# A hybrid mixer and MLP block on one Trainium2 core: two pairs of activation sums kept in SBUF, and another order of the steps at gate/up's begin

## The reference, cut to what matters

```python
D_MODEL, SEQ, D_FF = 2048, 512, 5632
h = rmsnorm(x, norm_mix)
proj = h @ w_in                       # then an SSD mixer, a sparse attention, a short conv
x = x + concatenate([y_ssd, y_att, y_sc]) @ w_out
h2 = rmsnorm(x, norm_ffn)
g = causal_dwconv(h2 @ ffn_w_gate, ffn_conv_w)        # width 3
x = x + (silu(g) * (h2 @ ffn_w_up)) @ ffn_w_down
# rmsnorm(x, g) = x * rsqrt(mean(x * x) + 1e-6) * g
```

## Time and profile before

| | us |
|---|---|
| median of 3 runs | 2159.3 (2154.16 to 2162.18) |
| the profiled execution | 2157.02, of it span 2155.2 |
| TensorE busy | 2124.2 |
| VectorE busy | 1495.8 |
| GpSimd busy | 1294.1 |
| ScalarE busy | 1009.0 |

### The profile page before, as it was taken

One profiled execution on the slowest core, in us unless ns is written; L12 is line 12 of the kernel. 1 busy time (PEld: TensorE's weight loads), 2 busy tenths in 40 slices (PEclk: granted clock), 3 DMA queues, 4 the chain that ended last, 5 costly groups with the idle time before them and its releaser, 6 DMA issues.

```text
span 2155.2 us, 36413 instructions
## 1 busy us (share of the span) xinstructions
PE 2124.2 (99%) x12484; PEld 1844.4 (86%) x12484; DVE 1495.8 (69%) x2530; ACT 1009.0 (47%) x1474; POOL 1294.1 (60%) x730
## 2 busy tenths in 40 slices
PE   8999999999999999999999999999999899999999
PEld 6777777887888887888888888888888889999999
DVE  6489565677763226888888888888888756566665
ACT  6343334434333445545555555455555444444444
POOL 4445334454554655667767767677677566666565
PEclk9999999999999999999999999999999999999999
DMA  5324223333334543353544544545445885566544
GB/s 194 86 79 120 66 69 98 94 105 91 100 103 126 147 142 127 124 170 132 172 154 141 165 151 147 169 133 175 149 141 169 320 278 178 176 219 203 188 125 143
DMA packets 153613, 316.22 MB, mean 147 GB/s; under 512 B 13176, under 2 KB 57912, under 8 KB 153496
## 3 DMA queue, kind: packets, MB, share of 16 engines
q1 hardware_dynamic: 103552, 252.23, 36.2%
q10 hardware_dynamic: 49944, 62.45, 9.2%
HBM read 265.31 MB, written 49.18 MB: 146 GB/s over the span
## 4 chain that ended last, share of the span: by engine, by line
PE 87%; DVE 8%; DMA 2%; issue 1%; ACT 1%; POOL 0%; ACTq 0%; SPq 0%; DVEq 0%; POOLq 0%
PE ps L846 26%; PE ps L845 13%; PE ps L657 9%; PE ps L659 8%; PE ps L658 8%; PE ps L852 6%; PE ps L854 6%; PE ps L853 6%; DMA act_lo<-tlo 1%; DVE work L1402 1%; DVE work L1401 1%; DVE work L1305 1%; PE ps L753 1%; PE ps L739 0%; DVE work L1304 0%
## 5 line engine op out<-in xcount | busy, mean ns | idle before, releaser
L846 PE MATMUL ps<-comb,fhi 128*128 128x512 f32 x2464 | 862.1, 394 | 0.0
L612 POOL TENSOR_TENSOR flo<-raw,fhi 128x1024 fp32r<-128x1024 f32 (+2 forms) x252 | 486.5, 1935 | 376.1 <-ACT fhi L1160 372.6
L845 PE MATMUL ps<-comb,flo 128*128 128x256 f32 x2464 | 693.5, 281 | 4.7 <-DVE ps L1737 3.3
L582 POOL TENSOR_TENSOR wlo<-raw,whi 128x512 fp32r<-128x512 f32 x260 | 375.7, 1458 | 393.4 <-ACT whi L959 342.7
L846 PEld LDWEIGHTS ps<-comb,fhi 128*128 128x128 f32 x2464 | 462.3, 188 | 105.4 <-issue 0.2
L845 PEld LDWEIGHTS ps<-comb,flo 128*128 128x128 f32 x2464 | 466.2, 189 | 8.6 <-issue 4.2
L612 POOL TENSOR_TENSOR flo<-sum,fhi 128x1024 fp32r<-128x1024 f32 (+2 forms) x168 | 323.4, 1931 | 51.4 <-ACT fhi L1160 49.6
L1160 ACT ACTIVATE fhi<-ps 128x1024 fp32r<-128x1024 f32 (+2 forms) x168 | 141.6, 843 | 414.3 <-DVE ps L1620 258.9
L852 PE MATMUL ps<-comb,fhi 128*128 128x256 f32 x1120 | 319.2, 285 | 10.5 <-POOL flo L612 6.5
L657 PE MATMUL ps<-hhi,whi 128*128 128x512 f32 x784 | 319.5, 407 | 3.2 <-DVE hlo L1542 3.2
L854 PE MATMUL ps<-comb,fhi 128*128 128x256 f32 x1120 | 318.6, 284 | 0.0
(11 more groups left out here) (223 smaller groups left out, 3082.8 us busy)
## 6 DMA issues: line engine op xcount, KB each, us to landing
raw<-w_gu SPq DMA_DIRECT2D x176, 512.0 KB, 3.7
raw<-w_in SPq DMA_DIRECT2D x196, 256.0 KB, 3.1
raw<-w_dn SPq DMA_DIRECT2D x96, 256.0 KB, 3.1
raw<-w_dn SPq DMA_DIRECT2D x64, 320.0 KB, 3.0
act_hi<-thi ACTq DMA_DIRECT2D x22, 896.0 KB, 4.2
act_lo<-tlo ACTq DMA_DIRECT2D x22, 896.0 KB, 8.3
raw<-w_out SPq DMA_DIRECT2D x64, 256.0 KB, 3.2
comb<-act_hi SPq DMA_DIRECT2D x28, 512.0 KB, 3.9
```

Source lines behind the costliest of these rows:

```text
L582: nc.gpsimd.tensor_tensor(wlo[:, slot % NW, 0:width], raw[:, slot % NRAW, 0:width], whi[:, slot % NW, 0:width].bitcast(F32), ALU.subtract) ...
L612: nc.gpsimd.tensor_tensor(flo[s][:, 0:w], src[:, 0:w], fhi[s][:, 0:w].bitcast(F32), ALU.subtract).then_inc(f_lo_pool, 1)
L845: nc.tensor.matmul(dst[:, 0:HT], flo[s][:, w], both[:, HI, :], start=fresh and k == 0, stop=False, skip_group_check=True)
L846: ins = nc.tensor.matmul(dst, fhi[s][:, w], both, start=False, stop=k == n - 1, skip_group_check=True)
```

## The change

At gate/up's begin:
- the Newton step keeps its intermediate in the PSUM bank `MLP`, where its input lies, in place of `upv`; the wait for the stored x2 tiles moves from there to just ahead of L1735;
- the activation table of Ln and Exp is loaded after the high part of position 3 of unit 0, six instructions earlier;
- the splits of the last tile are cut in two: T2 alone, then the weight sum S2 of unit 0 (position 2), then T3 and T4, on ScalarE and on VectorE. The semaphore counts of GpSimd's `low_h2` and of TensorE's position 4 follow.

Pairs 20 and 21:
- chunk 0 is made of pairs 0, 1, 2 and 20, chunk 1 of 3, 4, 5, 21 and 6; the others follow (`PAIRS`), and the weights are laid out in the same order;
- pair 20 stays in `thi` and `tlo` through chunk 0, and TensorE reads it there; pair 21 is split straight into slot 7 of `comb` and `comb6`, and is there for chunk 1. Neither is stored nor loaded, nor is a landed store waited for in unit 45. The loads of chunks 0 and 1 bring 3 pairs in place of 4 beside `fifth`;
- as `thi` and `tlo` are in use longer, the x2 tiles 12 and 13 go to `x2d` (where `gpad` was), 14 to `upv` and 15 to `sqsum`; `load_x2(6)` and `load_x2(7)` wait for the last activation in place of the last stores, and are three DMAs in place of two.

```diff
-PAIR0 = [0, 4, 9, 13, 18]
+PAIRS = [[0, 1, 2, 20], [3, 4, 5, 21, 6], [7, 8, 9, 10], [11, 12, 13, 14, 15], [16, 17, 18, 19]]
...
+        def pieces(c, b):
+            half, pairs = 4 * (c % 2), PAIRS[c]
+            run = [m for m in pairs[:4] if m < FP - 2]
+            found = [(block_of(b)[:, part, half:half + len(run), :], store[b, :, run[0]:run[0] + len(run), :])
+                     for part, store in ((HI, act_hi), (LO, act_lo))]
+            if len(pairs) == 5:
+                found += [(fifth[2 * b + part][:, :], store[b, :, pairs[4], :]) for part, store in ((HI, act_hi), (LO, act_lo))]
+            return found
...
+                if p == NPAIR - 1:
+                    sp_.dma_start(upv[:, :], x2_rows[2 * p]).then_inc(x2_loaded[p], 16)
+                    sp_.dma_start(sqsum[:, :], x2_rows[2 * p + 1]).then_inc(x2_loaded[p], 16)
+                    return
...
                 if u == FT + 4:
-                    sp_.wait_ge(t_hi_stored, 16 * FP)
-                    sp_.wait_ge(t_lo_stored, 16 * FP)
+                    sp_.wait_ge(f_act, FT)
                     load_x2(6)
                     load_x2(7)
...
-                    pool.wait_ge(h2_hi, 3 * m + 3)
+                    pool.wait_ge(h2_hi, 3 * m + (4 if d == KT - 1 else 3))
...
                     pool.wait_ge(t_hi, m + 1)
+                    if n == FT + 1:
+                        last = act[(FP - 1) % 2]
+                        nc.gpsimd.tensor_tensor(comb[:, :, LO, 7, :], last[:, 1:7, :], comb[:, :, HI, 7, :].bitcast(F32), ALU.subtract)
+                        nc.gpsimd.tensor_tensor(comb6[:, LO, 7, :], last[:, 7, :], comb6[:, HI, 7, :].bitcast(F32),
+                                                ALU.subtract).then_inc(t_lo, 1)
+                        return
                     if not isinstance(n, int) or m > 0:
                         pool.wait_ge(t_lo_stored, 16 * m)
...
-                    if not gate_up(u) and k == 4:
+                    if k == 4:
                         high, low = fifth[2 * b][:, :], fifth[2 * b + 1][:, :]
+                    elif u < FT + NPAIR and k == 3:
+                        high, low = thi[:, b, :], tlo[:, b, :]
...
+                if first:
+                    pe.wait_ge(h2_lo_t, FK + 1)
...
+                    if v in (0, NPAIR) and pos == 0:
+                        pe.wait_ge(t_lo, FP - 1 + c)
...
+                    if d == KT - 1:
+                        sc.wait_ge(h2_t, d + 1)
+                        A(comb[:, T2, HI, m, :], hst[:, T2 + 1, :], ACT.Copy).then_inc(h2_hi, 1)
+                        sc.wait_ge(sum2_ready, 1)
+                        high_unit(0, 2, wide(LEFT))
+                        sc.wait_ge(h2_t, d + 2)
+                        A(comb[:, T3:B22, HI, m, :], hst[:, T3 + 1:B22 + 1, :], ACT.Copy).then_inc(h2_hi, 1)
...
                 high_unit(n, 3, raw12)
+                if n == 0:
+                    nc.scalar.preload_act_table_set("natural_log_exp_and_others")
...
+                    if n == FT + 1:
+                        last = act[(FP - 1) % 2]
+                        A(comb[:, :, HI, 7, :], last[:, 1:7, :], ACT.Copy)
+                        A(comb6[:, HI, 7, :], last[:, 7, :], ACT.Copy).then_inc(t_hi, 1)
...
-                if lane(n) % 2 == 0 and (not isinstance(n, int) or 4 <= n <= FT + 2):
+                if lane(n) % 2 == 0 and (not isinstance(n, int) or 4 <= n < FT):
...
+                if d == KT - 1:
+                    ve.wait_ge(h2_hi, 3 * m + 2)
+                    V.tensor_tensor(comb[:, T2, LO, m, :], hst[:, T2 + 1, :], comb[:, T2, HI, m, :].bitcast(F32), ALU.subtract).then_inc(h2_lo_t, 1)
+                    low_s2(0)
+                    ve.wait_ge(h2_hi, 3 * m + 3)
+                    V.tensor_tensor(comb[:, T3:B22, LO, m, :], hst[:, T3 + 1:B22 + 1, :], comb[:, T3:B22, HI, m, :].bitcast(F32),
+                                    ALU.subtract).then_inc(h2_lo_t, 1)
+                    return
...
                 if first:
-                    for i in range(4):
-                        ve.wait_ge(x2_stored[i], 16 * (KT // 4))
                     ve.wait_ge(r2_r0, 1)
-                    newton(sqsum[:, :], upv[:, :], bank(MLP), D)
+                    newton(sqsum[:, :], bank(MLP), bank(MLP), D)
```

64 lines of the change are left out of this document (37 added, 27 removed).

## The result

The changed kernel takes 2138.1 us, median of 6 runs (2136.7 to 2142.2). Six runs of the kernel before, taken beside it, have a median of 2159.8 us (2154.2 to 2162.2). The ratio is 0.991, with an interval of 0.990 to 0.992: faster by 0.9%. The forecast was 2140.7 us with a range of 2135 to 2151.

The account below looks back on a forecast made before the run. TensorE, busy in 99% of the span, bounds the kernel; its waits and low clock could give 20.4 us. Gains of 5.8 us at gate/up's begin and 12.8 at down take the median from 2159.3 to 2140.7 us, range 2135 to 2151.

Parts of the forecast that it names:

- Position 2: Gate/up's begin, unit 0: TensorE's 1.31 us wait for `low_s2` shrinks to at most 0.3 us, about 1.2 us gained.
- The table load: Gate/up's begin, ScalarE: moving the 1.28 us load from ahead of Ln gains 0 to 1.28 us, taken as 0.9.
- The clock at the begin: Gate/up's begin, 815 to 855 us: the 1.6 us lost to a clock of 0.96 goes with the waits.
- (a): Unit 44: load waits of 1.85 us (position 5) and 2.1 us (position 6); only 0.7 us is left, at position 6.
- (b): Unit 45, position 5: the 1.47 us wait for a low part, laid to the landing of pair 20's store, goes.
- (c): Unit 46: the 0.64 us wait behind GpSimd's low part of pair 21 goes, with 1 us to spare.
- (d): Unit 47: the 4.44 us wait behind `copy_a21`'s late weight block goes, the block coming 6.3 us or more earlier.
- transfers would still end last: Rival at the transition to down: only half of the 14.2 us comes back, 2146.4 us; chance 0.17.
- Newton would give little: Rival at gate/up's begin: Newton's instructions stay blocked or the load lands on the same path, 2145.0 us; chance 0.08.
- the traffic was not the cause: Rival at the transition to down: issue order or GpSimd is late instead, 2152.5 us; chance 0.08.
- The slower case: Rival in units 45 to 49: x2 loads clog the queues, 19 us of delay plus 6 of clock, 2166 us; chance 0.05.
- Weight blocks within 5 us: Sign that the forecast holds: in units 45 to 47 the weight blocks land within 5 us.

Follow-up runs that it names:

- newton_only: The kernel before with only the Newton step's intermediate in PSUM and its wait for stored x2 tiles moved; 2151.6 us, ratio 0.998.
- after: The changed kernel with all edits, against the kernel before; 2138.1 us, ratio 0.991.
- before: The kernel without the change, run beside the changed one; median 2159.8 us.
- after_newton_sbuf: The changed kernel with the Newton intermediate back in SBUF (upv) and the wait for stored x2 tiles back ahead of it; 2139.7 us, ratio 0.992.
- after_with_stores: The changed kernel with the four stores of pairs 20 and 21 added back, which nothing reads or waits for; 2143.8 us, ratio 0.995.
- after_x2_later: The changed kernel with two x2 tile loads (1 MB) moved from unit 45 to unit 46 of SyncE's queue; 2135.6 us, ratio 0.991.
- pairs_only: The kernel before with only the edits on pairs 20 and 21, nothing of gate/up's begin; 2144.1 us, ratio 0.994.

## Why the prediction was right, point by point

**The bound.** TensorE's waits and its clock, 20.4 us in all, were said to be all that can be won. The two places gave 19.0. The kernel's median moved by 21.7, more than the 20.4; the untouched stretches and the choice of the profiled executions make up the difference.

**Position 2.** Forecast: at most 0.3 us of the 1.31 left. Measured: none, with 0.6 us to spare; newton_only against after gives 25.2 - 24.0 = 1.2 us for splits and load together, as was said for the splits alone.

**The Newton step.** Forecast 2.1 us for the chain, measured 2.16. The reason, GpSimd and two SBUF operands, held in the traces with the old form (before, after_newton_sbuf) and in those with the new one (after, newton_only).

**The table load** was sized at 0.9 of 1.28 us. It was worth all 1.3: in before's trace ScalarE does not idle between the last high part and the load, nor between the load and Ln, and in after's the last high part and Ln start 0.95 us apart. The 0.9 was too low because I counted gaps in front of instructions that the load would not have to wait for.

**The wait left at position 6 of unit 0**, 0.4 us, is not there. Table load and Newton each came out a little better than costed.

**The clock at the begin** was 1.6 us, and newton_only measures it at 4.94 - 3.34 = 1.60. The doubt, that such a figure counts a part twice, was not needed there. In down the windows priced it too low: the second low stretch began before the window of 1745 to 1775, as the window below shows (7 us at 0.51). Of its 3.4 us some 1.1 lie within the wait of 4.44 us and cost nothing; with the 1.65 of the first stretch that leaves 4.0 us, where 3.7 was forecast.

```profile
1742.00:1749.00 7.00, 4.82 (x23) 4.82 (x24) 3.68 (x7) 2.89 (x6) 3.74 (x3) 0.51 1.03 386
```

**The low part of T3 and T4** was said to be held up by GpSimd, 0.7 us, in slack. It lasts 1.26 us (L1636), two thirds of 0.96 would be 0.64; GpSimd's pair beside it lasts 1.89 where it lasted 1.59 before. The hold-up is 0.6 us, and no one waits for it.

**Units 44 to 47.** (a) 0.7 us of 4.0 was to be left, and it is 0.88, at position 6 as said. (b) The wait went, but the step's reason was half of it. I laid 1.47 us of TensorE's wait to the landing of pair 20's store, and treated the weight block as next late. after_with_stores has no wait for the landing and the same loss, since the weight block is late by as much: both are readings of one backlog, and only the bytes have a price. The "5 MB less" was too much as well: up to unit 45 the stores of pair 20 (1.8 MB), the smaller loads of chunk 0 (1.8 MB) and one or two positions of chunk 1 (0.26 MB each) make 4.2 MB at most. (c) Pair 21's low part was to be covered with 1 us to spare, and TensorE waits 0.47 us there. Of that miss of 1.5 us two terms are on the trace: GpSimd's two instructions take 4.25 us and not 4.1, and `copy_a21`, ahead, waits 0.65 us for its block. Behind it GpSimd works without a break up to the low part that TensorE waits for, so without the late block the wait of 0.47 us would not be there; the other 0.7 us of the miss stays open, and no run isolates any of it. The absence of the wait in after_x2_later says nothing on it: counted from the first matmul of down, GpSimd starts on pair 21 at 20.79 us there and at 20.86 in after, and it is TensorE that comes 0.6 us later. (d) Of the wait of 4.44 us 0.34 is left. The block for `copy_a21` still comes late (2.79 us of idle time), and TensorE is covered but for that. Left in all were 1.4 us by forecast, 1.69 by trace (0.88, 0.47 and 0.34).

**That down meets the forecast to the tenth is luck.** The sum of waits and clock was 14.2 us and should have been 10.5 + 4.0 = 14.5, and 1.7 us are left in place of 1.4: two misses of 0.3 us that cancel. The mechanism holds, the bytes above all. Of the steps, the reason of (b) was half wrong and (c) was missed by 1.5 us, of which only 0.47 show, as the rest was spare.

**Costed at nothing**, and rightly: TensorE does not wait ahead of unit 44, nor in any unit behind 47, so the split of pair 20, the third x2 DMA and the first unit of chunk 1 have no price.

**The rivals.** That transfers would still end last, and that Newton would give little, fell with pairs_only and newton_only. That the traffic was not the cause fell with after_with_stores: 9.3 us back for 3.67 MB of stores. The slower case, x2 loads that clog the queues, rested on one row, the low rate of 158 GB/s for a microsecond, and that row was misread. The trace of after has the same kind of stretch, from 1687 to 1688:

```profile
DMA packets 39, 0.08 MB, mean 80 GB/s; under 512 B 0, under 2 KB 0, under 8 KB 39
```

It is a time in which the queues had run empty: no packet starts from 1686.6 to 1687.4. The next transfers were issued from 1686.50 on; their first packets start at 1687.5 on SyncE's queue and at 1688.2 on ScalarE's. In before's trace it is the same place of the program: the transfers issued from 1693.05 on were only beginning, and those before them were running out. A low rate is evidence of clogging only if something is waiting in the queue.

**The signs.** As they were listed: Newton at 0.7 each, the clock at 1.00 from 840 on, no wait for GpSimd over 1 us, and 7.35 MB less in the span (7.3 said) came true. "Weight blocks within 5 us" did not: their median is 3.7 from 1685 to 1760, but of the 14 issued from 1690 to 1727 eight land after 5.7 to 8.2 us. Nor was that without harm: the block issued at 1694.92 (8.0 us) is the one for which `copy_a21` waits 0.65 us, the one at 1717.61 (6.8 us) that of the 2.79 us, and behind them stand TensorE's waits of 0.47 and 0.34 us. No sign of being wrong came.
